# Decay rows of the layer-2 mixers: mask on VectorE earlier, own sum as the bias of ScalarE's exponentials

## The reference, cut to what matters

```python
def lower_exp_diff(cs):
    n = cs.shape[-1]
    tril = jnp.tril(jnp.ones((n, n), dtype=bool))
    diff = cs[..., :, None] - cs[..., None, :]
    return jnp.where(tril, jnp.exp(jnp.where(tril, diff, 0.0)), 0.0)
...
    lmat = lower_exp_diff(a_cs)
    scores = jnp.einsum('bclhn,bcshn->bhcls', cc, bc) * lmat
...
    decay = lower_exp_diff(gc)
    strict = jnp.tril(jnp.einsum('bhcid,bhcjd->bhcij', kbeta, kc) * decay, -1)
    sol = lax.linalg.triangular_solve(strict, rhs, left_side=True, lower=True, unit_diagonal=True)
    qk = jnp.einsum('bhcid,bhcjd->bhcij', qc, kc) * decay
```

## Time and profile before

| what | us |
|---|---|
| time, median of 3 runs | 2251.5 |
| lowest and highest of them | 2251.28, 2252.94 |
| span of the profiled execution | 2258.5 |
| own time of the profiled execution beside its span | not listed |
| PE busy in the span | 2216.4 (98%) |
| DVE busy | 1581.9 (70%) |
| ACT busy | 914.2 (40%) |
| POOL busy | 263.5 (12%) |

### The profile page before, as it was taken

The page is one execution under the profiler, slowest core; times in us unless marked ns, Lnnn a source line. Parts: engine busy times, 40 slices in busy tenths (PEclk is TensorE's granted clock), DMA queues, the critical chain, the costliest instruction groups (busy, mean ns, idle before and its releaser), DMA issues. The chain is left out here.

```text
span 2258.5 us, 34288 instructions
## 1 busy us (share of the span) xinstructions
PE 2216.4 (98%) x13052; PEld 1823.0 (81%) x13052; DVE 1581.9 (70%) x2212; ACT 914.2 (40%) x1672; POOL 263.5 (12%) x266
## 2 busy tenths in 40 slices
PE   8999999999999999999999989999999999999997
PEld 7888888888888887887877777887888888888886
DVE  5657678876665545657687788887798777765557
ACT  5443544343343321243344445555533333324444
POOL 0222232100000000001232222322020000000000
PEclk9999999999999999999999989999999999999999
DMA  4111111144333264433233442323235444448655
GB/s 152 47 38 58 37 56 38 66 147 157 116 114 111 86 261 175 150 111 122 85 112 112 150 141 72 107 93 112 96 131 191 163 158 163 158 156 299 214 181 184
DMA packets 106952, 289.06 MB, mean 128 GB/s; under 512 B 9692, under 2 KB 35388, under 8 KB 102332
## 3 DMA queue, kind: packets, MB, share of 16 engines
q1 hardware_dynamic: 106812, 287.14, 36.2%
HBM read 205.01 MB, written 82.10 MB: 127 GB/s over the span
## 5 line engine op out<-in xcount | busy, mean ns | idle before, releaser
L124 PE MATMUL psG<-h_hi,w_hi 128*128 128x512 f32 (+1 forms) x624 | 164.4, 395 | 2.1 <-DVE features_T L1875 1.6
L124 PE MATMUL psG<-h_hi,w_lo 128*128 128x512 f32 (+1 forms) x624 | 161.6, 391 | 0.0
L124 PE MATMUL psG<-h_lo,w_hi 128*128 128x512 f32 (+1 forms) x624 | 161.4, 392 | 0.0
L455 POOL TENSOR_TENSOR sb_w<-sb_left 128x128 f32<-128x128 f32 (+3 forms) x96 | 96.9, 1014 | 320.3 <-DVE sb_left L582 320.3
L124 PEld LDWEIGHTS psG<-h_hi,w_hi 128*128 128x128 f32 x624 | 109.9, 188 | 23.7 <-DVE features_T L1875 2.9
L124 PEld LDWEIGHTS psG<-h_hi,w_lo 128*128 128x128 f32 x624 | 111.4, 188 | 20.2 <-DVE w_lo L155 0.2
L124 PEld LDWEIGHTS psG<-h_lo,w_hi 128*128 128x128 f32 x624 | 111.1, 188 | 20.1 <-issue 0.5
L582 DVE TENSOR_TENSOR_SCAN sb_left<-sb_left 128x128 f32<-128x128 f32 (+3 forms) x96 | 102.7, 1078 | 2.1 <-ACT sb_left L468 1.4
L150 ACT CAST w_hi<-w_raw 128x1024 fp32r<-128x1024 f32 x48 | 50.3, 1049 | 120.0 <-PE psG L124 61.7
L155 DVE TENSOR_TENSOR w_lo<-w_raw,w_hi 128x1024 fp32r<-128x1024 f32 x48 | 58.6, 1222 | 55.0 <-ACT w_hi L150 55.0
L2024 POOL TENSOR_TENSOR features_T<-m_bias_both 128x512 f32<-128x512 f32 x10 | 16.8, 1675 | 680.3 <-DMA m_bias_both<-in_proj_pairs 633.0
(11 more groups left out here) (657 smaller groups left out, 5949.8 us busy)
## 6 DMA issues: line engine op xcount, KB each, us to landing
w_raw<-in_units SPq DMA_DIRECT2D x76, 512.0 KB, 4.3
w_raw<-hidden_blocks SPq DMA_DIRECT2D x77, 256.0 KB, 2.9
merge_gates<-features_T SPq DMA_DIRECT2D x12, 1024.0 KB, 6.7
merge_gates<-merge_gates SPq DMA_DIRECT2D x12, 1024.0 KB, 4.8
features<-features_T SPq DMA_DIRECT2D x24, 512.0 KB, 3.8
w_spare<-in_units SPq DMA_DIRECT2D x22, 512.0 KB, 4.4
down_sums<-w_spare SPq DMA_DIRECT2D x22, 512.0 KB, 3.3
hidden_blocks<-features_T SPq DMA_DIRECT2D x11, 1024.0 KB, 3.9
```

What stands on the lines that cost most here:

```text
L124: return pe.matmul(out, lhs, rhs, start=first, stop=last, skip_group_check=True)
L455: pool.tensor_tensor(w, left_chunk(S, 1), left_chunk(S), ALU.subtract).then_inc(w_ready, 1)
```

## The change

On VectorE, dsub and dmask go. In their place, ahead of level 4, one addition (dm) puts the mask on the loaded rows; it waits for the load of the rows. The minimum with 0 is left out, since the mask alone brings the upper part to -1e30. GpSimd makes the negated own sums of the 12 heads (nac, 128 x 12) behind the copy of the parameters. On ScalarE, twelve exponentials of 128 columns, one for each head, take that column as their bias: the four GDN heads first (LG), then the eight SSD heads (LS). In tile 0 they stay behind the PTR copy; in tiles 1 to 7 they move up, from ahead of `joined` to directly behind `product(8)`, ahead of `high_weights(4, 6)`, pc1 and `product(16)`. The readers nc, nt and qkd wait for LG, sd0 and sd1 for LS.

```diff
-        PT, PSC, zero = sb("par", [P, PEND]), sb("state_decay", [P, 2]), sb("zero", [P, 1])
+        PT, NAC, PSC, zero = sb("par", [P, PEND]), sb("minus_decay_sums", [P, NH]), sb("state_decay", [P, 2]), sb("zero", [P, 1])
...
                     poolF.done("par", g.tensor_copy(PT[:], prm[:, n, :]))
+                    poolF.done("nac", g.tensor_tensor(NAC[:], zero[:].to_broadcast([P, NH]), prm[:, n, PACS:PACS + NH], ALU.subtract))
...
                 if chain:
                     product(8)
+                def decayed():
+
+                    vectF.wait(a, "dm", n)
+                    poolF.wait(a, "nac", n)
+                    for h in (*range(SH, NH), *range(SH)):
+                        ins = a.activation(DEC[:, h], DEC[:, h], ACT.Exp, bias=NAC[:, h:h + 1])
+                        if h in (SH - 1, NH - 1):
+                            scalL.done("LS" if h < SH else "LG", ins)
+
+                if front and n:
+                    decayed()
                 if n == 1:
                     high_weights(4, 6)
...
                 if chain:
                     product(32)
                     upper()
-                def decayed():
-                    vectF.wait(a, "dmask", n)
-                    scalL.done("L", a.activation(DEC[:], DEC[:], ACT.Exp))
-
-                if front and n:
-                    decayed()
                 if chain:
                     joined()
...
                 if n == 2:
                     low_weights(5, 6)
+                if front:
+                    v.wait_ge(dec_here, 16 * n + 16)
+                    vectF.done("dm", tt(DEC[:], DEC[:], over(MSK[:, 0, :], NH), ALU.add))
                 level(4)
...
-                if front:
-                    v.wait_ge(dec_here, 16 * n + 16)
-                    vectF.done("dsub", tt(DEC[:], DEC[:], per(PT[:, PACS:PACS + NH], NH, P), ALU.subtract))
-                    vectF.wait(v, "dsub", n)
-                    vectF.done("dmask", v.scalar_tensor_tensor(DEC[:], DEC[:], 0.0, over(MSK[:, 0, :], NH), ALU.min, ALU.add))
...
                 if front:
-                    scalL.wait(v, "L", n)
+                    scalL.wait(v, "LG", n)
                     tensF.wait(v, "qk", n)
...
-                    scalL.wait(v, "L", n)
+                    scalL.wait(v, "LS", n)
                     tensF.wait(v, "sc", n)
```

More of the change, by code:

```diff
@@ L2262, in layer2_mixers @@
         scalG = Steps(sem("scalar_chain"), "T2 yq0 yq1 yln yexp T4 mtm T8 T16 T32 vu0 vu1 va vo1 vo0 T64 wt vn osq oln oexp")
-        vectF = Steps(sem("vector_front"), "ss ssc nqk kb qg swab mx mx2 ngm sdif dsub dmask nc0 nc1 nc2 nc3 nt qkd sd0 sd1 den rden "
+        vectF = Steps(sem("vector_front"), "ss ssc dm nqk kb qg swab mx mx2 ngm sdif nc0 nc1 nc2 nc3 nt qkd sd0 sd1 den rden "
                                            "yo yx att st1 y yz st2")
-        scalQ, scalL, tensY = Steps(sem("scalar_queries"), "qt"), Steps(sem("scalar_decays"), "L"), Steps(sem("tensor_off"), "yo")
+        scalQ, scalL, tensY = Steps(sem("scalar_queries"), "qt"), Steps(sem("scalar_decays"), "LG LS"), Steps(sem("tensor_off"), "yo")
         vectX, vectN = Steps(sem("vector_xdt"), "xdt xdec"), Steps(sem("vector_blocks"), "m1 vt1 v0")
@@ L2268, in layer2_mixers @@
         vectD, vectH = Steps(sem("vector_state"), "s0 s1 s2 s3"), Steps(sem("vector_turned"), "mglo")
-        poolF = Steps(sem("gpsimd_front"), "par keep0 keep1 xd kprev nm vbt vprev")
+        poolF = Steps(sem("gpsimd_front"), "par nac keep0 keep1 xd kprev nm vbt vprev")
         poolG = Steps(sem("gpsimd_chain"), "kbg kd pes gzn qgt qkdc")
```

## The result

The changed kernel takes 2262.68 us (median of six runs, 2262.04 to 2263.53) against 2252.22 beside it: a ratio of 1.0035, 95% interval 1.0022 to 1.0048, slower by more than the 0.2%. (A ratio here is an estimate over the runs of both kernels and not the quotient of two medians, which would be 1.0046.) The forecast was 2259.2, range 2250 to 2266.

A forecast was written before the change was run, and what follows sets the result against it. TensorE was taken to bound tiles 3 on, VectorE 1304 to 1334, TensorE's halved clock 1334 to 1355. 1.1 + 1.6 + 1.0 + 1.5 + 2.5 = 7.7 on 2251.5 gave 2259.2 us, range 2250 to 2266.

The forecast's parts named there:

- one of the signs of being wrong: No wait at dm in tile 0, exponentials 0.2 apart, gapless TensorE in tiles 3 to 7, or clock 1.00 from 1334 to 1355.
- the bias row: Softmax exponential with a bias, 256 columns, 504 ns; used to price the twelve ScalarE exponentials at 3.5 us a tile.
- Tile 0, +1.1: dm waits for the first rows and delays the passes queued behind it, the softmax exponentials and block copies: +1.1 us.
- Tile 1, +1.6: dm makes T8 2.0 late; exponentials and casts make the T16 copy 4.2 late, delaying qk and X64: +1.6 us.
- Tile 2, +1.0: dm behind a weight subtraction makes V4 and qk 2.2 late, partly given back behind qk: +1.0 us, between +0.7 and +2.2.
- The clock, +2.5: New TensorE gaps in tile 1 make its clock fall earlier, halving speed from qk to X64: 0 to 5.2, taken +2.5 us.
- Tiles 3 to 7, 5 x 0.3: T8 is 0.3 late in each full tile behind dm, with xd arriving during it: +1.5 us, range 0.5 to 3.
- the exponentials nearly fit: In tiles 3 to 7 the exponentials need 3.5 us against a ScalarE gap of 3.06, with 0.5 to spare at qk.
- (a): Rival: the clock holds through tile 1, so 1334 to 1355 shrinks by 10.2: -5.0 in all, 2246.5 us; chance 0.17.
- (b): Rival: only the late load and part of the rest count, the clock falling where it did: +2.6, 2254.1 us; chance 0.25.
- (c): Rival: ScalarE late in every full tile, qt 0.6 late for qk five times: +3.0, 2262.2 us; chance 0.15.
- VectorE sets the pace: In tiles 0 and 1, from 1304 to 1334, VectorE, busy 29.07 of 30 us, was taken to bound the kernel.

The follow-up runs named there:

- the second profile: The changed kernel, unedited, run and profiled a second time; 2261.98 us, ratio 1.0035.
- the base: The kernel before, unchanged, profiled a second time, at 2252.46 us; its eight runs have median 2255.55, ratio 1.0010.
- late kernel: Changed kernel's arithmetic, but mask added at the old place in all tiles, eight exponentials ahead of the joining copies, four behind the root; 2257.94 us, ratio 1.0010.
- with the first tiles late: Tiles 0 to 2 as in the late kernel, tiles 3 to 7 as in the changed kernel; 2259.12 us, ratio 1.0020.
- with the negation added: The kernel before plus GpSimd's negation of the own sums, whose result nobody reads; 2256.97 us, ratio 1.0008.
- the late kernel with the negation behind: The late kernel, with GpSimd's negation moved behind its copies, just ahead of the skip product; 2255.21 us, ratio 1.0004.

## Why the prediction was right, and where its sizes were off

The sign holds and 2262.68 lies in the range; 7.7 was forecast and about 10.4 came (9.0 by the second profile). Most mechanisms named were there: the wait for the first rows, dm ahead of V4 with GpSimd in its way, late T8, an earlier fall of the clock, and a constant loss in the full tiles.

That the sum came so near is in part luck. The prediction said that it works out differences to the execution it had read. Against that execution the span grew by only 2.3 (2258.5 to 2260.8), and tile 1 became 5.0 shorter (42.84 to 37.84). Up to X64 its account of tile 1 holds in size: X64 is 4.3 late without tile 0's share, and 1.6 + 2.5 had been forecast. But it left the stretch from 1334 to 1355 at half its clock, and there the changed kernel ran at 0.99, in its second profile at 1.00, which is one of the signs of being wrong that it named. The sum fits the median because executions near the median do not have that low stretch either. By its steps:

- **Prices of the added work.** dm 1.75 (said 1.70 to 1.72); an exponential 0.396 us and twelve in 3.61 (said 0.40 and 3.5); the negation 0.2 (said so). The choice of the bias row over the copy's overlap was right.
- **Tile 0, +1.1.** Mis-sized: 2.6 against the execution it was worked out from (3.2 against the base), and undoing it gave 2.7. The rows landed 7.0 after the issue, not 6.5, so dm ran at 1294.15, not 1293.55. swab was then 2.1 late, where 1.34 was said. The rest is the step "the softmax exponentials and PTR wait for that chain", which moved PTR by as much as swab: PTR was 2.8 late. TensorE had stood for 2.33 us, and its clock was 0.79 in 1296 to 1304, where the base has 1.00; that this is why the rest came later is argued and not shown.
- **Tile 1, +1.6.** Its first link holds: T8 late by dm (2.5 more wait in the second profile, said 2.0; of that 0.85 is GpSimd, near the upper bound of 0.8, not the 0.3 taken). The second link, exponentials and casts delaying the T16 copy by 4.2 and this the qk product, fails: the copy without the casts waited for TensorE, and TensorE listed no wait for that copy in either profile. The old waits behind T8 (0.18, 0.95, 0.36 and 0.53 in the base) did go, except for 0.60 of the 0.95 at qk in the second profile. All listed waits of tile 1 behind its first transposes come to 4.11 in the base, 3.94 in the changed kernel and 5.40 in its second profile, so in place of +1.6 the waits give -0.2 and +1.3.
- **Tile 2, +1.0.** In waits -0.6: 4.15 in the base, about 3.6 after, with T8's 2.92 taking the place of later ones (three are gone, and qk's falls from 0.96 to 0.34).
- **The clock, +2.5.** The term that was mis-sized most. What tiles 1 and 2 are longer, less what their waits grew, is 4.4 and 2.2 in the first profile of the changed kernel and 1.4 and 2.1 in the second: 6.7 and 3.4, an estimate of what the clock took. The step failed in counting one fall, in tile 1, and only the work from qk to X64. There are two falls, and the one in tile 1 begins ahead of T8 in the first profile (1321.0, T8 at 1325.28) and just behind it in the second (1326.2, T8 at 1325.64), in both well ahead of qk.
- **Tiles 3 to 7, 5 x 0.3.** 5 x 0.33, right in size and half right in cause. T8 was to lose 0.1 to dm and 0.2 to xd; it loses 0.18, with dm undisturbed. The other half is the step "the exponentials nearly fit": qt and qk did have room, but the copy out of bank 7, which ended that very gap of 3.06, was not followed to the product that needs the bank. The Trainium skill's page "SBUF — State Buffer", section "Who interferes with whom", which I set aside for the row of the 1024-column sum, was right here: dm began first and kept 1.75, xd took 1.76. The row did not speak against it either, I misread it: in the trace of before GpSimd's copy m_v_prev (1453.92, 0.85 us) had begun ahead of that sum (1454.4) and had 0.3 us left, which roughly fits the 0.2 more that the sum took, and the GpSimd product behind took 1.59 in place of 0.60.
- **Rivals.** (a) had nothing to win back in the median: the clock already holds from 1334 to 1355 in an execution near it. Its condition, a clock of 1.00 there, came about, and the time still rose. The fault lies ahead of it: the prediction saw 7.0 us between the span of the profiled execution and the median (8.8 between the times) and did not ask in which stretch they lay. (b) fell with the clock. (c) missed its place: qt was in time, the product's copy was not.
- **"VectorE sets the pace."** This was read from its 29.07 busy us of 30 in tiles 0 and 1. With one VectorE pass of 1.7 us less and the mask added at the old place, tile 1 takes 33.9 to 34.1 (late kernel and its variants) against 33.57 in the base: the pass taken away was not what TensorE waited for.

What is shown by undoing it: that the places and not the arithmetic cost (ratio 1.0010 in place of 1.0035), tile 0 (2.7 by one execution; at least 2.2 lie between all that add the mask early there and all that do not), xd's share of T8 in both tiles (0.85 each), the copy behind the exponentials (0.15 a tile), and, with the first tiles late, T8's wait in tile 1 (0.17). What is argued: that T8's long wait makes the clock fall in tile 1. For it: in all six profiles with dm early in tile 1 (waits of 0.98 to 2.69 at T8) it falls there, and in the seven with a wait of 0.17 or 0.18, the first profile of before left out, it does not. Against it: in three of the six the clock was already low before that wait, so there something else ahead of T8 must have taken part, and in that first profile, with 0.18, it fell at 1334. What makes it fall stays open, and with it the 3.4 to 6.7 us of the loss put down to the clock.

## What to carry to other kernels

Making the busiest engine lighter is worth nothing of itself: left at its place in the queue, the lighter work gave no gain that shows. And it can cost when it is moved: here a pass was moved from where it hid to in front of the block chain that TensorE waits for, and ahead of a load that had not landed. For every stretch of ScalarE or VectorE that looks free, look at what ends the gap and who waits for that, not at the length of the gap alone. And before a forecast is made as a difference to one profiled execution, find out in which stretch that execution differs from the median.

## What the hardware showed that I had not expected

Two operations of VectorE and GpSimd on SBUF do not share the loss: with starts 0.03 us apart, the first ran at 1.21 (VectorE's remainder) and the other at 2.08 in place of 1.04; with GpSimd 0.05 ahead, it kept 1.04 and VectorE took 2.06. Whether TensorE's clock falls in tile 2 was not settled by the waits from T8 to qk: with the same ones (0.40 at T8, 1.1 at the level-16 blocks, 0.95 at qk) it held in the base (36.41) and fell with the negation added (38.14) and in the late kernel with the negation behind (40.74), a spread of 4.3 us. And an operand that would be late at the higher level need not be at the lower: with the clock at 1.2 GHz and the casts of tile 1 moved away, ScalarE waited 2.00 us for TensorE at T16, not the other way round.
